# Two-layer attention and expert kernel: due times of expert rows, and the rows TensorE takes beside the last routings

## What is computed

```python
def block(xb):                       # 128 tokens
    q = einsum('td,dhc->thc', xb, w_q)
    s1, s2 = scores of q's halves against 128 keys each, for 4 heads
    v1, i1 = top_k(s1, 8); v2, i2 = top_k(s2, 8)
    top, pos = top_k(all 64 sums v1 + v2, 8)          # per head
    idx = the chosen pair of keys -> one of 16384 experts
    g = softmax(top)
    act = gelu(einsum('thkd,td->thk', u_tab[idx], xb))
    return einsum('thk,thkd->td', g * act, v_tab[idx])
```

## Time and profile before

| | |
|---|---|
| time, median of 3 runs | 2858.8 us (2851.58 to 2866.93) |
| profiled execution, its own time | 2838.57 us |
| its span, first to last instruction | 2836.8 us |
| mean granted TensorE clock | 0.935 of 2.4 GHz |
| DMA moved | 776.95 MB, mean 274 GB/s |

### The profile page before, as it was taken

One profiled execution on the slowest core, in us unless ns is written; L12 is line 12 of the kernel. 1 busy time (PEld: TensorE's weight loads), 2 busy tenths in 40 slices (PEclk: granted clock), 3 DMA queues, 4 the chain that ended last, 5 costly groups with the idle time before them and its releaser, 6 DMA issues.

```text
span 2836.8 us, 30116 instructions
## 1 busy us (share of the span) xinstructions
PE 2420.2 (85%) x10600; PEld 1468.1 (52%) x10600; DVE 1951.1 (69%) x4015; ACT 784.1 (28%) x1555; POOL 1239.7 (44%) x1028
## 2 busy tenths in 40 slices
PE   8998998988899999898988887998989999784036
PEld 4664476565445357656654565574445357552012
DVE  0122245588988866668887886588988866678865
ACT  2243222213344332311342212213344333201001
POOL 0000023354656423445564544255665423555775
PEclk9998999998989999999998998998999999997669
DMA  3323258787888766978997889787888766996998
GB/s 143 104 69 102 89 194 345 269 310 254 309 288 299 266 214 254 370 296 300 352 343 268 331 332 390 261 287 274 311 297 312 266 208 227 379 366 245 363 347 323
DMA packets 224181, 776.95 MB, mean 274 GB/s; under 512 B 23200, under 2 KB 39712, under 8 KB 219552
## 3 DMA queue, kind: packets, MB, share of 16 engines
q0 software_dynamic: 147456, 536.94, 51.7%
q1 hardware_dynamic: 73696, 227.80, 22.6%
q10 hardware_dynamic: 2880, 10.31, 0.9%
HBM read 766.56 MB, written 8.39 MB: 273 GB/s over the span
## 4 chain that ended last, share of the span: by engine, by line
PE 39%; DVE 23%; DMA 14%; POOL 12%; issue 9%; ACT 2%; DVEq 0%; ACTq 0%; POOLq 0%
PE ps L1056 10%; POOL rows L840 9%; DMA rows<-in_table_u,idx 8%; DVE x L1535 7%; PE ps L900 6%; PE ps L1089 4%; DMA rows<-in_table_v,idx 4%; PE ps L931 4%; DVE rows L1520 3%; PE ps L886 3%; PE ps L984 3%; PE ps L1124 2%; POOL xT L840 2%; PE ps L1150 2%; DVE scratch L1777 1%
## 5 line engine op out<-in xcount | busy, mean ns | idle before, releaser
L840 POOL DMA_INDIRECT rows<-in_table_u,idx x462 | 561.5, 1215 | 1075.7 <-DVE idx L1643 558.6
L1056 PE MATMUL ps<-xT,wring 128*128 128x256 f32 x3072 | 762.8, 397 | 45.8 <-DMA wring<-in_merge 22.7
L840 POOL DMA_INDIRECT rows<-in_table_v,idx x436 | 530.9, 1218 | 454.1 <-DVE x L1535 348.5
L1056 PEld LDWEIGHTS ps<-xT,wring 128*128 128x128 f32 x3072 | 581.8, 196 | 231.6 <-issue 79.6
L1520 DVE CUSTOM_DVE_ANT_0 rows<-rows,x 128x1024 f32<-128x1024 f32 x462 | 555.0, 1224 | 133.3 <-DMA rows<-in_table_u,idx 129.0
L1535 DVE SCALAR_TENSOR_TENSOR x<-rows,wts,x 128x1024 f32<-128x1024 f32 x416 | 533.5, 1283 | 76.8 <-DMA rows<-in_table_v,idx 55.8
L1089 PE MATMUL ps<-KA,QA 33*128 33x512 f32 (+7 forms) x576 | 251.1, 533 | 48.0 <-DVE negm L1777 23.3
L1389 ACT ACTIVATE scratch<-scratch,negm 128x640 f32<-128x640 f32 (+7 forms) x192 | 143.5, 747 | 501.2 <-DVE negm L1777 501.1
L900 PE MATMUL ps<-wring,G 128*128 128x512 f32 x384 | 184.5, 616 | 12.4 <-DVE G L1678 6.3
L1777 DVE CUSTOM_DVE_ANT_0 scratch<-ps,cst 128x128 f32<-128x128 f32 (+3 forms) x192 | 86.8, 454 | 136.6 <-PE ps L1089 136.1
L886 PE MATMUL ps<-oT,wring 128*128 128x256 f32 x384 | 121.7, 452 | 62.6 <-DVE G L1673 60.2
(11 more groups left out here) (209 smaller groups left out, 2930.3 us busy)
## 6 DMA issues: line engine op xcount, KB each, us to landing
wring<-in_merge SPq DMA_DIRECT2D x216, 512.0 KB, 6.9
wring<-in_w_out_h SPq DMA_DIRECT2D x48, 512.0 KB, 7.1
wring<-in_w_query SPq DMA_DIRECT2D x32, 512.0 KB, 4.7
G<-in_w_query SPq DMA_DIRECT2D x12, 1024.0 KB, 9.9
G<-in_x SPq DMA_DIRECT2D x16, 512.0 KB, 5.9
G<-in_ln SPq DMA_DIRECT2D x8, 1024.0 KB, 6.9
G<-x_mid SPq DMA_DIRECT2D x16, 512.0 KB, 7.2
rows<-in_table_u,idx POOLq DMA_INDIRECT x462, 7.6
```

What stands on the lines that cost most here:

```text
L840: pool.indirect_dma_start(row_slot(n), None, tab_u if table == "u" else tab_v, bass.IndirectOffsetOnAxis(ap=idx[:, GT * (g % 2) + t, e:e + ...
L1056: mm = pe.matmul(gate_bank(p)[:, SW * n:SW * (n + 1)], w[:, lo:lo + P], xT[:, kc, SW * (p // HALF_GATES):SW * (p // HALF_GATES + 1)], star ...
```

## The change

The planner's clock of landed rows now holds for every group, rows come due over 0.88 instead of 0.8 of a group's time, and a row is taken to land every 1.9 us instead of 1.75. These are numbers of the planner: they move rows between steps and add none. Apart from that, block 26 joins the blocks that TensorE shares: it takes ten rows from the first one of `SHARES["rest"]` on, every third after them, and in block 27 every third from its third row on (10 instead of 16). The places that set and wait for the weights follow.

```diff
--- before.py
+++ after.py
@@ -367,7 +367,7 @@
                 due = started
                 if own + 1 < NG and routed:
                     due = max(due, routed[own] + SPREAD * k * (routed[own + 1] - routed[own]) / (NS * SECTION_STEPS))
-                if own == NG - 1:
+                if own == NG - 1 or True:
                     due = max(due, landed)
                 if max(busy, due) + EXPERT_US > now + ahead:
                     break
@@ -387,7 +387,7 @@
 
 
 EXPERT_US, EXPERT_AHEAD, TIGHT_AHEAD = 1.33, 3.0, -0.5
-SPREAD, ROUTED, ROW_US = .8, [], 1.75
+SPREAD, ROUTED, ROW_US = .88, [], 1.9
 for _ in range(3):
     SHARES, ROUTED = expert_shares(ROUTED)
 
@@ -412,8 +412,8 @@
 
 
 SUM_BLOCKS = [b for b, (sec, table, t) in enumerate(BLOCKS)
-              if table == "v" and (sec == len(SECTIONS) - 1 or sec == len(SECTIONS) - 2 and t % ST == 1)]
-DIAGS, ROUTING_ROWS = 4, 8
+              if table == "v" and sec >= len(SECTIONS) - 2 and NEXP * (b + 1) > SHARES["rest"].start + 3]
+EARLY_SUMS, DIAGS, ROUTING_ROWS = len(SUM_BLOCKS) - ST, 4, 10
 
 
 def by_tensor(n):
@@ -421,8 +421,8 @@
 
 
     b, e = n // NEXP, n % NEXP
-    if b == SUM_BLOCKS[0]:
-        return e < ROUTING_ROWS or e % 3 == 2
+    if b in SUM_BLOCKS[:EARLY_SUMS]:
+        return e < NEXP - 1 and (0 <= n - SHARES["rest"].start < ROUTING_ROWS or e % 3 == 2 and n > SHARES["rest"].start)
     return b in SUM_BLOCKS and e % 2 == 0
 
 
@@ -1242,7 +1242,7 @@
                     store(b - 1)
                 if by_tensor(at):
                     te, t = rows_read_by(at)[1], BLOCKS[b][2]
-                    if e == 0:
+                    if e == first_and_last(b, True)[0]:
                         act.wait_ge(weights_set, sums_before(b) + 1)
                     if te > DIAGS:
                         act.wait_ge(rows_summed, te - DIAGS)
@@ -1489,7 +1489,7 @@
                 after(v.reciprocal(gel[:, :], gel[:, :]))
                 after(v.tensor_tensor(wts[:, t, :], dots[:, t, :], gel[:, :], ALU.mult))
                 ins = v.tensor_tensor(wts[:, t, :], wts[:, t, :], gw[:, GT * (g % 2) + t, :], ALU.mult)
-                if g == NG - 1 and t >= 1:
+                if g == NG - 1 and t >= GT - len(SUM_BLOCKS):
                     ins.then_inc(weights_set, 1)
                 else:
                     after(ins)
```

## The result

The changed kernel takes 2840.2 us (median of 13 runs, 2824.8 to 2855.9), the kernel before 2866.2 us in 13 runs beside it (2851.6 to 2884.4). The ratio is 0.991, with a 95% interval of 0.9885 to 0.9935: 19 to 33 us less. The experiments ran on three chips, called A, B and C here; the changed kernel ran on two of them, B and C, again: 0.9869 (0.9845 to 0.9892) on B and 0.9924 (0.9899 to 0.9949) on C. The profiled execution of before that the prediction reads (2838.6 us) was quicker than each of those 13 runs, so the spans of the first two profiles (2836.8 and 2839.6 us) say nothing of the gain. Of the timed executions in the experiments two are left out of the ratios, one of TensorE's rows alone on A (2881 us at a granted clock of 0.899) and one of the kernel before on B (8275 us).

A forecast was written before the change was run, and what follows sets the result against it. TensorE's order of work, busy 85%, bounds the kernel until its last match step, then fetches do. Terms -7 - 16 - 2 + 1 = -24 us from the 2858.8 us median give 2834.8 us, range 2810 to 2857.

The forecast's parts named there:

- The tail: Behind the last routings: TensorE takes rows 841 to 850 at 2.0 us each, moving the end by -7 us.
- The rival of half clock: Behind TensorE's last match: its ten rows take 3.75 us each, row 866 goes 10 us later; -7 in all, 2852 us; 8%.
- The heads: Group heads: DVE earlier at zc; -6 us in group 1, -8 in group 3, -2 at 1634 us; sum -16.
- The ends: Merges ending groups: -5 us each at 1181 and 2467 us, +8 at 1762 us; together -2 us.
- Five rows more cost 6.5 us (1.3 each) to 10 us: Third merge, 1762 us: 29 rows instead of 24 follow on DVE; taken as +8 us on a 14.27 us wait.
- my bound of 12 us growth: Third merge: prediction wrong if the wait there grows by more than 12 us.
- one of the signs that I had named for being wrong: Prediction wrong if waits for weights take the place of the heads' waits; no size given.
- The middle: Middle of groups 1 and 3: held-back rows go ahead of section 0's first route, other steps stay the same; +1 us.
- term 4: Groups 1 and 3: four held-back rows ahead of softplus line 1720, nothing to +3 us in each; +1 us in all.
- the last of my signs for being wrong: Prediction wrong if TensorE waits for line 1720 around the route steps of groups 1 and 3.
- the first rival: Heads and merges: waits only change their name; heads and ends give -5, total -9, 2850 us; 19%.
- The rival on the slower side: Group 2's first routes to the 1762 us merge: 13 held-back rows paid in full, +26 there, +19 in all, 2878 us; 9%.

The follow-up runs named there:

- the old rule for group 2: Changed kernel, but rows 256 to 511 planned as before (0.8 of the group's time, no clock of landed rows): 0.9918 on A, 0.9914 on C against the kernel before.

## Why the prediction came out

The time, 2834.8 us or -24, was near: -26, on C -22 and on B -37. Its parts were not.

**The tail** was under-sized, -14.4 us for -7. A row costs TensorE 1.76 us and not 2.0; the 2.0 came from two rows (4.16 us) that followed closely on an idle time, and the next two in the same trace took 3.60. That moved row 866 by 8.7 us instead of 7.2. At row 869 the ten rows themselves gain 13.6 us (21.4 less 7.8), of which the planner's three more rows behind the last routes take back 4.9 there, though not visibly at the end (262.4 and 261.9 us of tail for the planner alone, 260.4 and 266.9 for the kernel before). Row 917 is only 9 to 10 us earlier (79.5 us after the last `idx`, before 88.4 and 89.4). The other 5 to 6 us come behind row 917, where nothing was changed: from its issue to the end it is 172 and 178 us in two executions of before, 166, 166 and 177 in three of the change, and 161 to 176 in the others. So a part of the surplus is spread or has a cause that I don't know. The rival of half clock fell: the granted clock is 1.00 over the ten rows. The Trainium skill (TensorE: Matmul & The Clock Gate, Part 1), which says that activity releases the throttle, agrees with that stretch.

**The heads** are right in place and sign: both waits for `negm_c` went, and the two stretches shrank by 11 and 6 us, the first beyond my 6: TensorE was granted half clock for 31 to 51 us there in before's order and for 20 to 31 in the changed one. The wait at 1634 us fell by about 1 us over the executions (from 4.6 to 3.4), where I had 2.

**The ends.** The merge at 2467 us came out as priced: 7.4 us of waits for 12.8 in the first profiles, the last stretch 4.5 us shorter over the executions. That at 1181 us gave some 3 us and not 5: the 7.19 us that I read were the most of four executions (2.6 to 7.2), and the changed order has 2.2 to 3.4 us in four and none above 0.3 in two. At the third merge "Five rows more cost 6.5 us (1.3 each) to 10 us" is too much and not the whole mechanism: DVE was done with its rows about 2 us later, and another 2.5 or so came from weights, through the block end among those rows, a store and SP's queue. The wait went from 14.3 to 17.7 us, inside my bound of 12 us growth; but that it was a wait for weights is one of the signs that I had named for being wrong. I had costed the moved rows and not what block 15's end releases; that SP's order was unchanged hid that SP's waits were not. By the Trainium skill (DMA: Bandwidth & Descriptors, Queues, rings and completion order) queues share the DMA engines by turns, from which I worked out slower rows; here the weights were late mainly because they had been issued 16 us later after the last `idx` than before, and no run measures what the taking of turns would add.

**The middle** is the step that failed. I wrote that the other steps of groups 1 and 3 "keep the same rows between them, only 10 or 15 numbers lower, and stay the same". A block's end is tied to a row's number, so lower numbers move it to other steps: in group 1 ahead of `aug`, where the wait went from 2.64 to 5.15 us and the 16 matmuls behind it took 5.76 us instead of 3.63 at the lower clock. The wait is 5.15 or 5.16 us in all six executions of the changed order; what follows it is not so steady, and the stretch from 877 to 1023 us, 6.8 us longer on average, was no longer on chip B (148.3 us, before 148.4 there). The other 4.4 us in the middle of group 1 lie between 785 and 877 us, where TensorE is idle for as long as before (5.5 us for 5.1); what they come from is open. In group 3 the wait for `aug` at 2309 us is 4.9 us for 2.6.

Group 3 also has the place that term 4 put at nothing to +3 us, and TensorE waits there, the last of my signs for being wrong. The changed kernel (timelines of PE, then DVE):

```profile
2343.80 0.59 PE L1158 MATMUL ps<-cst 128*128 128x512 bf16 x1 [3.07 <-DVE scratch L1725]
...
2337.88 1.28 DVE L1535 SCALAR_TENSOR_TENSOR x<-rows,wts,x 128x1024 f32<-128x1024 f32 x1 [2.76 <-DMA rows<-in_table_v,idx]
2341.01 1.28 DVE L1535 SCALAR_TENSOR_TENSOR x<-rows,wts,x 128x1024 f32<-128x1024 f32 x1 [1.84 <-DMA rows<-in_table_v,idx]
2342.32 0.69 DVE L1720 SCALAR_TENSOR_TENSOR scratch<-ps,scratch 128x512 f32<-128x512 f32 x1
```

In the kernel before TensorE comes to the same step without a wait (timelines of DVE, then PE):

```profile
2316.76 0.69 DVE L1725 TENSOR_TENSOR scratch<-scratch,cst 128x512 f32<-128x512 f32 x1
...
2322.89 0.38 PE L1158 MATMUL ps<-cst 128*128 128x512 bf16 x1
```

The slack was 5.4 us there (2317.45 done at DVE, 2322.89 needed). I had counted only what the rows cost DVE in work, 1.37 us each, and two of them now wait 2.76 and 1.84 us for their landing ahead of line 1720. All six executions of the changed order have this wait (2.3 to 4.2 us), the four of before's order and the two with only the old rule for group 2 have none, and the stretch of the place, 2305 to 2452 us, is 4.6 us longer on average. In the table the middles give back 11 and 9.5 us, 21 of the 25 us that the four other stretches ahead of the tail had won.

So the first rival, that waits only change their name, is what happened to the planner's part: 0.9997 and 0.9986 by itself, 2 to 3 us, where I had -17 us and that rival -2 (-5 + 2 + 1). That the whole came out near my time is luck in part: the tail's surplus stood in for what the planner did not give. Its 19% was too low; its number for the whole, -9, missed because of the tail. The rival on the slower side did not occur: holding the 13 rows back in group 2 cost 13 us in that stretch, against the old rule, and about nothing in the whole.

## What to carry over

When a planner moves work, list what is tied to each item's number (a block's finish, a store, and who in another queue waits for that store), not only how many items stand ahead of a wait. When a trace names what ended a wait, look whether another engine would have ended it hardly earlier before calling that the price. A wait taken off a nearly busy engine is only a gain once the sum over the whole period shows it; measure the halves of a change on one chip, and cut several executions at the same marks before believing a place. Handing rows to an engine that stands idle behind its last work was worth more than all the retiming.

## Not expected

**TensorE's instructions came late in one stretch, in some executions.** The 128 matmuls of the query step in the head of group 2 (line 931) take 27.9 us from first to last in the first profile of before and in all four on chip B, the changed kernel's among them. In the change's first profile they take 46.6 us, and on A and C 45.8 to 47.1 in five executions and 38.9 to 40.5 in three. Timeline of PE in the first profile of the change:

```profile
1274.30 0.58 PE L931 MATMUL ps<-G,scratch 128*128 128x256 f32 x1 [1.52 <-issue]
1275.69 0.58 PE L931 MATMUL ps<-G,scratch 128*128 128x256 f32 x1 [0.81 <-issue]
1278.49 1.50 PE L931 MATMUL ps<-G,scratch 128*128 128x256 f32 x2 [2.21 <-issue]
```

and of the same program on chip B:

```profile
1254.77 3.62 PE L931 MATMUL ps<-G,scratch 128*128 128x256 f32 x16
1258.23 3.62 PE L931 MATMUL ps<-G 128*128 128x256 f32 x16
```

No engine and no transfer is named for the idle time; the mean granted clock over the 128 matmuls is 0.78 in the first profile of the change and 1.00 where they take 27.9 us. On which chip the first two profiles ran is not on record. The 18 us are near the difference of the kernel before between the chips (2845 us on B, 2866 on A and 2860 on C). That these are the same thing was not tried, nor what holds the instructions back.

**Waits of a few us mostly come with half clock, but not all.** In the changed kernel the granted clock is 0.69 from 1007 to 1016 us, around the end of the `aug` wait of 5.15 us, 0.81 from 1180 to 1189 us, behind the wait of 2.34 us, and 0.69 from 1775 to 1784 us, behind the 17.72 us; in the kernel before it is 0.67 from 635 to 644 us, behind 6.61 us, but 1.00 from 1010 to 1019 us, behind the 2.64 us for `aug`. The planner's half alone runs at a mean clock no higher than before (0.9256 against 0.9265, and 0.9277 against 0.9283), although it has fewer long waits.
